# First attention: the division by the softmax sums moves from the output to the probabilities, and from VectorE to GpSimd

## The reference

```python
s = jnp.where(valid[:, None, None, :, :], s, -jnp.inf)
sink = jnp.broadcast_to(sinks.astype(jnp.float32).reshape(1, 1, ATTN_KV_HEADS, ATTN_GROUPS, 1, 1), s.shape[:-1] + (1,))
probs = jax.nn.softmax(jnp.concatenate([s, sink], axis=-1), axis=-1)[..., :-1]
o = jnp.einsum('bnhgqk,bnkhd->bnqhgd', probs.astype(v.dtype), vw)
```

## Time and profile before

| | us |
|---|---|
| median of 3 runs | 1982.31 (1981.1 to 1982.51) |
| the profiled execution | 1981.18 |
| its span, first to last instruction | 1979.4 |
| TensorE matmul busy | 1898.3 (96%) |
| VectorE busy | 1191.0 (60%) |
| ScalarE busy | 801.1 (40%) |
| GpSimd busy | 549.8 (28%) |
| mean granted TensorE clock | 0.982 of full |

### The profile page before, as it was taken

One profiled execution on the slowest core, in us unless ns is written; L12 is line 12 of the kernel. 1 busy time (PEld: TensorE's weight loads), 2 busy tenths in 40 slices (PEclk: granted clock), 3 DMA queues, 4 the chain that ended last, 5 costly groups with the idle time before them and its releaser, 6 DMA issues.

```text
span 1979.4 us, 24272 instructions
## 1 busy us (share of the span) xinstructions
PE 1898.3 (96%) x9486; PEld 1557.3 (79%) x9486; DVE 1191.0 (60%) x1790; ACT 801.1 (40%) x1418; POOL 549.8 (28%) x554
## 2 busy tenths in 40 slices
PE   8999999999997999999999999989999998899999
PEld 6788888766776888887788887878988897667687
DVE  4578435455688667667777788446435348466641
ACT  6665212455553333343333344442211136455521
POOL 0031015640256565530000023651532134011100
PEclk9999999999998999999999999999999999899999
DMA  5153432211224544559656510123101313311133
GB/s 155 43 150 106 142 83 91 81 43 54 75 75 132 171 147 146 174 195 391 239 180 212 175 39 28 46 57 128 43 23 43 107 56 141 107 33 32 43 95 97
DMA packets 226186, 216.76 MB, mean 110 GB/s; under 512 B 37320, under 2 KB 166600, under 8 KB 225560
## 3 DMA queue, kind: packets, MB, share of 16 engines
q1 hardware_dynamic: 226072, 215.21, 33.9%
HBM read 154.31 MB, written 60.87 MB: 109 GB/s over the span
## 4 chain that ended last, share of the span: by engine, by line
PE 73%; DVE 11%; ACT 5%; POOL 4%; issue 3%; DMA 2%; SPq 1%; DVEq 0%; POOLq 0%; ACTq 0%
PE ps L361 10%; PE ps L362 9%; PE ps L363 9%; PE ps L1816 5%; PE ps L1817 4%; PE ps L2195 4%; PE ps L1818 4%; PE ps L2197 4%; PE ps L2196 4%; PE ps L3512 4%; PE ps L378 3%; PE ps L596 2%; PE ps L3413 1%; PE ps L3501 1%; PE ps L3502 1%
## 5 line engine op out<-in xcount | busy, mean ns | idle before, releaser
L361 PE MATMUL ps<-xh,whi 128*128 128x512 f32 (+2 forms) x1176 | 466.2, 396 | 9.5 <-DVE wlo L330 5.5
L362 PE MATMUL ps<-xl,whi 128*128 128x512 f32 (+2 forms) x1176 | 450.4, 383 | 0.0
L363 PE MATMUL ps<-xh,wlo 128*128 128x512 f32 (+2 forms) x1176 | 450.0, 383 | 0.0
L361 PEld LDWEIGHTS ps<-xh,whi 128*128 128x128 f32 x1176 | 224.2, 191 | 56.3 <-issue 8.5
L363 PEld LDWEIGHTS ps<-xh,wlo 128*128 128x128 f32 x1176 | 223.7, 190 | 40.7
L362 PEld LDWEIGHTS ps<-xl,whi 128*128 128x128 f32 x1176 | 224.1, 191 | 34.0 <-issue 0.2
L1816 PE MATMUL ps<-oph,wsh 128*128 128x512 f32 x448 | 177.3, 396 | 14.8 <-DVE stu L1928 8.1
L2195 PE MATMUL ps<-dnh_b,dnh_a 128*128 128x512 f32 x448 | 176.1, 393 | 6.9 <-DVE dn_b L2221 6.9
L1817 PE MATMUL ps<-opl,wsh 128*128 128x512 f32 x448 | 176.1, 393 | 0.0
L2196 PE MATMUL ps<-dn_b,dnh_a 128*128 128x512 f32 x448 | 176.0, 393 | 0.0
L1818 PE MATMUL ps<-oph,wsl 128*128 128x512 f32 x448 | 176.0, 393 | 0.0
(11 more groups left out here) (501 smaller groups left out, 3473.0 us busy)
## 6 DMA issues: line engine op xcount, KB each, us to landing
dnr_b<-ff_d SPq DMA_DIRECT2D x28, 1024.0 KB, 8.0
dnr_a<-w_down SPq DMA_DIRECT2D x28, 1024.0 KB, 5.8
wraw<-w_in SPq DMA_DIRECT2D x47, 512.0 KB, 3.9
ff_d<-st SPq DMA_DIRECT2D x64, 256.0 KB, 5.2
ff_d<-stt SPq DMA_DIRECT2D x48, 256.0 KB, 5.1
upx<-w_up SPq DMA_DIRECT2D x16, 512.0 KB, 4.2
upy<-w_up SPq DMA_DIRECT2D x16, 512.0 KB, 5.5
xt<-x SPq DMA_DIRECT2D x8, 512.0 KB, 7.8
```

The lines of the kernel that those rows point to most:

```text
L361: pe.matmul(out, h, xh[:, xk, c0:c1_], start=(n == 0), stop=False)
L362: pe.matmul(out, h, xl[:, xk, c0:c1_], start=False, stop=False)
L363: mm = pe.matmul(out, l, xh[:, xk, c0:c1_], start=False, stop=(n == nk - 1))
```

## The change

GpSimd multiplies a block's probabilities with their reciprocal sums before they are turned, four instructions per block, in place, in the slot of step 5 and after the reciprocals. TensorE waits for each chunk's multiplication before it turns the chunk. The eight matmuls that spread the reciprocals, their bank and their copy go. The product with the values is then the output; ScalarE copies it to `tq` where it copied the spread reciprocals before, and VectorE's last multiplication goes. A lane takes 10 banks per block instead of 11.

```diff
             elif s in (6, 7):
-                w.wait_ge(*act_mx.at("aexp", i))
                 for c in (2 * s - 12, 2 * s - 11):
+                    w.wait_ge(*pool_mx.at("scaled", i, c))
                     p = take(w, lane, ("apT", i, c), (dve_mx if c % 2 else act_mx, ("apT", i, c)))
...
             elif s == 8:
-                p = take(w, lane, ("arT", i), (act_mx, ("arT", i)))
-                w.wait_ge(*dve_mx.at("arc", i))
-                rc = mx[i % 2][:, 32:40]
-                for sl in range(8):
-                    a = 64 * (sl % 2)
-                    t = pe.matmul(p[a:a + 64, 128 * (sl // 2):128 * (sl // 2) + 128], bc(rc[:, sl:sl + 1], [128, 64]), ident[:], start=True, stop=True)
-                t.then_inc(*pe_mx.up("arT", i))
-                p = take(w, lane, ("apv", i), (dve_mx, ("aout", i)))
+                p = take(w, lane, ("apv", i), (act_mx, ("aout", i)))
...
             elif s == 8:
-                w.wait_ge(*pe_mx.at("arT", i))
-                act.activation(tq[:, i, :], tile("arT", i), ACT.Copy).then_inc(*act_mx.up("arT", i))
+                w.wait_ge(*pe_mx.at("apv", i))
+                act.activation(tq[:, i, :], tile("apv", i), ACT.Copy).then_inc(*act_mx.up("aout", i))
...
-            elif s == 8:
-                w.wait_ge(*pe_mx.at("apv", i))
-                w.wait_ge(*act_mx.at("arT", i))
-                dve.tensor_tensor(tq[:, i, :], tq[:, i, :], tile("apv", i), ALU.mult).then_inc(*dve_mx.up("aout", i))
...
                 for b in range(4 * hf, 4 * hf + 4):
-                    w.wait_ge(*dve_mx.at("aout", b))
+                    w.wait_ge(*act_mx.at("aout", b))
...
         if kind == "rope":
             query_rope_pool(pool, w, k)
+        if kind == "attend" and hf == 5:
+            n = 128 if k == 0 else 256
+            rc = mx[k % 2][:, 32:40]
+            w.wait_ge(*dve_mx.at("arc", k))
+            for c in range(4):
+                d = score_pair(k, c, n)
+                pool.tensor_tensor(d, d, bc(rc[:, 2 * c:2 * c + 2].unsqueeze(2), [128, 2, n]), ALU.mult).then_inc(*pool_mx.up("scaled", k, c))
```

## The result

| | before | after |
|---|---|---|
| median, us | 1982.3 (4 runs) | 1996.9 (1995.87 to 2001.72, 4 runs) |
| ratio | | 1.008, 95% interval 1.0067 to 1.0092 |
| profiled execution / its span | 1981.18 / 1979.4 | 1995.98 / 1994.2 |
| mean granted TensorE clock | 0.982 | 0.982 |

Slower by 14.6 us between the medians, 0.8% by the ratio; forecast was 1997, 15 us. The profiled execution after was 1.75 us late before any changed instruction ran (the residual's first transposes start at 387.36 instead of 385.61; most of it arose in the first 25 us, around the input loads). It gave 1.8 us back behind the stage.

What follows compares the result with a forecast made beforehand. TensorE was taken to set the time. Its offsets of +12.8 us, 0.7 for the shared port and 1.5 for the clock sum to 15.0 us, giving 1997 us, range 1991 to 2002, chance 0.62.

Steps and rivals of the forecast that it cites:

- The queue: At block 6 the multiplications stand behind 17.9 us of rotations on GpSimd; TensorE stands 7.8 us, is 7.4 behind.
- Blocks 4 and 5 in front of it do not count: What TensorE loses or saves at these two blocks is taken up by its wait at block 6.
- The port: VectorE and GpSimd take turns on a shared port: +0.7 us behind block 1's reciprocal, elsewhere missed or slack.
- the list: TensorE's offset against the run before, followed from block 6 through 7, 0, 1, 2, 3 and tail: +12.8 us.
- The clock: The new stall of 7.8 us at block 6 should bring one slow-clock stretch: +1.5 us (0 to 3).
- The latency: Blocks whose transposes started at the end of their exponentials pay 2.0 to 2.4 us each, half-width block 0 0.9.
- The removal: Sixteen matmul records per block go from TensorE, 0.93 us each block, 7.4 us at most; nothing at block 6.
- The rings: PSUM bank rings turn by one; the 3.4 us stall goes, yet block 1 comes out even, +10.2.
- Queue harmless: Rival: rotations do not stand in the way, block 6 pays 1.0 instead of 7.4, no slow clock: 1989; chance 0.15.
- Contention: Rival: VectorE's traffic makes each GpSimd multiplication cost 1.5 us or more: 2004; chance 0.13.
- Faster: Rival: multiplications hide in slack TensorE has anyway, only the 0.93 us per block remain: 1976; chance 0.05.
- no change: Rival: savings and latency cancel, with half the latency and without the queue: 1982; chance 0.05.

Runs made afterwards that it cites:

- e1: Changed kernel with the rotations of blocks 0 to 3 spread over slots 5, 9, 12 and 17 instead of 6 and 7; 1989.8 us, ratio 1.0037.
- e8: Kernel before with only the rotations moved to the places they have in e1; 1982.1 us, ratio 0.9998.
- e2: Changed kernel without the 32 multiplications, division left out, TensorE waiting for the last exponential as before; 1978.1 us, ratio 0.9975.
- e12: Changed kernel without the multiplications, division left out, PSUM rings turned as before by skipping the reciprocals' bank; 1977.9 us, ratio 0.9981.
- e3: Changed kernel with the PSUM rings turned as before, skipping the bank the reciprocals had; 2000.6 us, ratio 1.0094.
- e4: As e1, but each multiplication covers only half of its chunk's columns; 1985.4 us, ratio 1.0014.
- e9: As e1, with sums and reciprocals in two parts on VectorE, heads 0 to 5 first, then 6 and 7; 1979.9 us, ratio 0.9993.
- the plan with the gap: Transposes of probabilities one slot later, rotations placed as in e1: changed kernel 1980.6 us, kernel before 1987.4 us.

## Why the prediction was right

**The queue.** Right, and shown by e1. The wait was 6.4 us instead of 7.8, since TensorE itself came 2.8 us later than I had it (442.69 - 6.39 - 1.75 = 434.6, forecast 431.8); what counts is where it ends, and that was 1.8 us later than forecast (offset 9.2 against 7.4). The step that failed is "Blocks 4 and 5 in front of it do not count": what makes block 5's reciprocal late moves the whole queue. Block 5's multiplications started at 417.33 - 1.75 = 415.6 where I had 413.85, and the cause is the port at block 4.

**The port.** The step that failed is "Elsewhere VectorE's work with two SBUF inputs misses the multiplications or delays chunks 2 and 3". At block 1, where I booked 0.7 us, four multiplications took 4.37 us instead of 4.03. The larger case is at block 4. Timeline of VectorE before, then after, then in e8:

```profile
400.29 1.29 DVE L1425 TENSOR_TENSOR tv<-tv,sso 128x512 f32<-128x512 f32 x2
...
413.55 0.20 DVE L1395 RECIPROCAL mx<-mx 128x8 f32<-128x8 f32 x1
```
```profile
402.04 3.02 DVE L1414 TENSOR_TENSOR tv<-tv,sso 128x512 f32<-128x512 f32 x2
...
416.41 0.60 DVE L1386 TENSOR_TENSOR mx<-mx 128x8 f32<-128x8 f32 x1 [4.76 <-ACT sc L1347]
417.05 0.20 DVE L1388 RECIPROCAL mx<-mx 128x8 f32<-128x8 f32 x1
```
```profile
402.12 1.29 DVE L1426 TENSOR_TENSOR tv<-tv,sso 128x512 f32<-128x512 f32 x2
...
415.80 0.20 DVE L1396 RECIPROCAL mx<-mx 128x8 f32<-128x8 f32 x1
```

Two VectorE products from SBUF took 3.02 us where they took 1.29 before, beside four multiplications (from 400.03) that took 4.49. Behind them in VectorE's order stand block 5's masks and maxima, so that its exponentials, its reciprocal and GpSimd's whole queue come late. The other suspect is the slow stretch from 398 to 402 (clock 0.57), in which the scores of block 5 come 1.6 us late. The runs hold the two apart; the last column is the reciprocal's start, counted from the residual's first transposes in each profile (385.61 before, 387.36 after, 387.44 in e8, 388.51 in e1):

| | multiplications at block 4 | clock ahead of block 4's transposes | the pair, us | block 5's reciprocal |
|---|---|---|---|---|
| before, e2, e12 | no | full | 1.28 to 1.29 | 27.9 to 28.0 |
| e8 | no | 0.51 | 1.29 | 28.4 |
| e1 | yes | full | 3.02 | 29.7 |
| changed kernel, e3 | yes | 0.57 and 0.60 | 3.02 | 29.7 |
| e4, half as long | yes | 0.56 | 1.47 | 28.3 |

The slow stretch alone costs 0.4 us, the port alone 1.75, both together no more than the port. That agrees with the contention that the Trainium skill states (GPSIMD Engine Reference, Specifications). Of my two terms behind the list, the port's was booked at 0.7 us and was worth at least 1.75.

**The clock.** Booked at 1.5 us behind block 6's stall; against e1 it was 1.15 there. The slow stretch from 398 to 402 cost nothing in the end, as the table shows. The one from 418 to 423 (0.66) made TensorE later at block 6, where it waits for GpSimd anyway.

**The sum.** That 15.0 met the measured 14.9 so closely is luck. 1.75 us at block 4 had no term and the clock was 0.35 too high; the list and the port at block 1, 13.5 together, thus came to some 12.0. Which of its steps were too high by how much is not resolved beyond what follows.

**The latency.** Right: 1.7 us of waiting at block 7 and 2.3 in its offset for the 2.4 forecast. From block 6 on it makes 9.6 us between e1 and e2 (see e2); my list has 2.4, 0.8, 2.0 and 2.9 us by name (the last with the late exponentials in it) and block 1's inside its "even". e4 and e9 show that it goes with the multiplications' time behind the last exponential, each with some of the port's loss in it. One multiplication took 1.04 us, as L817, and four without a break 4.03. By the Trainium skill (GPSIMD Engine Reference, Elementwise) I had estimated 1.11; the row was nearer. What I said the sum would rise by at 1.11, 1.5 us, was reckoned too high: 0.07 us more for each of the 14 full-width multiplications that my list has on the path makes 1.0.

**The removal.** Too large. The list lets five blocks gain (7, 0, 1, 2 and 3), apart from what I took back by waits; for e2 I expected seven, and 9 us from the removal by itself. e2 gives 3.9. In the changed kernel this hardly showed, for in e2's expectation gain and price were both too large by some 5 us (9 and 24 us against 3.9 and 18.8). That they cancel so nearly was not explained by a run.

**The rings.** I booked block 1 as even and so took the turned rings for worthless by themselves; e3 says they saved up to 3.7 us in the changed kernel. Within the list "even" and the port's 0.7 were right together (+0.7 from block 0 to block 1), for "even" already contained the turned rings; my reading of what it would be without them, the expectation of e3, failed.

**The rivals.** "Queue harmless" is excluded by the 6.4 us; as a kernel it is e1, at 1989.8 where it was priced at 1989. "Contention" as I priced it, 1.5 us for every multiplication, by the 1.04; but contention of the other kind, GpSimd holding up VectorE, is the 1.75 us that I missed. "Faster" and "no change" by the waits: behind block 6 only block 0's half-width transposes found next to no wait (0.24 us) without a change of the plan.

## What to carry to other kernels

Moving work to an idle engine is priced by two questions that its busy share does not answer: what stands in its queue when the data are ready, and whether the consumer has slack. Here 31 us of work (4.04 in seven blocks, 2.33 in the eighth) on an engine that was 80% idle cost 18.8 us, 7.1 by one group of instructions ahead in the queue and 11.7 by the rest, most of it because TensorE came for the result just when its input was ready, 1.75 because the new work held up VectorE through the port, ahead of that queue. A third question is therefore whom the engine slows while it works. And the answer belongs to the plan: in the plan with the gap the same change gains 6.8 us. The cheap mends were in the order of the work (the group moved, the reciprocals taken in two parts: 17 us together), and a removed instruction is only worth its time where the next wait is not already waiting.

## What the runs showed of the hardware

- VectorE's operations with two SBUF inputs and GpSimd's multiplications slow one another: 3.02 us instead of 1.29 for a pair on VectorE, 4.49 instead of 4.03 for four on GpSimd. Beside shorter multiplications (four in 2.32 us) the pair took 1.47. A 128x8 sum on VectorE took 0.60 instead of 0.17 us beside a GpSimd instruction, a reciprocal of the same size 0.20 as ever.
- A GpSimd product of 512 columns with a broadcast second operand takes 1.01 to 1.04 us, the low halves, with two full operands, 1.28 (L1477); a product of 256 columns with a broadcast one takes 0.58.
- The stretches at 1.2 GHz come and go with small changes: 398 to 402 in the kernel after (0.57), at the full 1.00 in e2, whose instructions up to there are the same but for the multiplications and the waits for them, and at 0.51 from 399 to 402 in e8, which has no multiplications. In the kernel before it lay from 390 to 394 (0.62). One profile a kernel does not tell how much of this changes from execution to execution.
